# Score products of cached sample keys with both operands split into high and low parts, four tiles to a step, and four groups of instructions in other places

## The reference

```
h = rmsnorm(x, g_mix);  z = h @ w_in           # all heads and gates in one projection
mlstm: 4 heads;  dilated attention (dsa): 3 groups of 2 heads;  moba: 6 heads of 64
sample sequence:  s = q @ concat(cached k, new k).T / 8 + bias;  o = softmax(s) @ concat(cached v, new v)
x = x + merge(branches) @ w_out;  x = x + SwiGLU(rmsnorm(x)) @ w_down;  y = rmsnorm(x)
```

## Time and profile before

| | |
|---|---|
| median of 3 runs | 998.3 us (997.5 to 999.62) |
| profiled execution | 997.17 us, of which span 995.4 us |
| TensorE busy, products / weight loads | 98% / 95% of the span |
| VectorE, ScalarE, GpSimd busy | 49%, 34%, 8% |
| HBM read and written | 98.00 MB and 15.45 MB, 114 GB/s over the span |
| mean granted TensorE clock | 0.998 |

### The profile page before, as it was taken

The page is one execution under the profiler, slowest core; times in us unless marked ns, Lnnn a source line. Parts: engine busy times, 40 slices in busy tenths (PEclk is TensorE's granted clock), DMA queues, the critical chain, the costliest instruction groups (busy, mean ns, idle before and its releaser), DMA issues.

```text
span 995.4 us, 18277 instructions
## 1 busy us (share of the span) xinstructions
PE 972.5 (98%) x7624; PEld 947.2 (95%) x7624; DVE 487.0 (49%) x886; ACT 337.5 (34%) x577; POOL 75.6 (8%) x106
## 2 busy tenths in 40 slices
PE   6999999999999999999999999999999999999998
PEld 5899989999889899999999999999999999999997
DVE  5735566444886122645355565555445555323232
ACT  7443233444553441322222342222222222222122
POOL 0100022011301100111113000000000000000000
PEclk9999999999999999999999999999999999999999
DMA  7586437322321764222222222222223222222302
GB/s 251 149 251 235 76 90 152 114 81 78 103 60 35 224 196 114 84 86 86 85 86 85 86 85 86 85 86 88 94 96 98 94 85 75 86 74 76 116 2 90
DMA packets 104909, 105.03 MB, mean 106 GB/s; under 512 B 11130, under 2 KB 101752, under 8 KB 104492
## 3 DMA queue, kind: packets, MB, share of 16 engines
q1 hardware_dynamic: 101224, 92.78, 30.3%
q0 software_dynamic: 3552, 11.08, 3.6%
...
HBM read 98.00 MB, written 15.45 MB: 114 GB/s over the span
## 4 chain that ended last, share of the span: by engine, by line
PE 89%; DVE 5%; issue 1%; ACT 1%; POOL 1%; SPq 1%; DMA 1%; ACTq 0%; DVEq 0%; POOLq 0%
PE acc L451 75%; PE acc L1108 2%; PE acc L1057 1%; PE acc L1033 1%; PE acc L1144 1%; POOL mt L830 1%; DVE w_lo L435 1%; PE acc L1091 1%; PE acc L911 1%; PE acc L900 1%; SPq L681 1%; PE acc L871 1%; PE acc L1017 1%; DVE h_lo L2069 1%; PE acc L1232 1%
## 5 line engine op out<-in xcount | busy, mean ns | idle before, releaser
L451 PE MATMUL acc<-h_hi,w_hi 128*128 128x256 f32 (+1 forms) x1520 | 465.1, 306 | 2.1 <-DVE w_lo L435 1.6
L451 PE MATMUL acc<-h_lo,w_hi 128*128 128x256 f32 (+1 forms) x1520 | 437.7, 288 | 0.0
L451 PE MATMUL acc<-h_hi,w_lo 128*128 128x256 f32 (+1 forms) x1520 | 435.8, 287 | 0.0
L451 PEld LDWEIGHTS acc<-h_hi,w_hi 128*128 128x128 f32 x1520 | 285.8, 188 | 10.3 <-issue 4.2
L430 ACT ACTIVATE w_hi<-raw 128x1024 fp32r<-128x1024 f32 x135 | 141.4, 1047 | 441.7 <-PE acc L451 441.6
L451 PEld LDWEIGHTS acc<-h_lo,w_hi 128*128 128x128 f32 x1520 | 286.1, 188 | 4.8 <-issue 2.4
L451 PEld LDWEIGHTS acc<-h_hi,w_lo 128*128 128x128 f32 x1520 | 286.1, 188 | 0.0
L435 DVE TENSOR_TENSOR w_lo<-raw,w_hi 128x1024 fp32r<-128x1024 f32 x135 | 165.3, 1225 | 112.5 <-ACT w_hi L430 107.8
L451 PE MATMUL acc<-s_hi,w_hi 128*128 128x256 f32 (+1 forms) x352 | 101.6, 288 | 0.0
L451 PE MATMUL acc<-s_lo,w_hi 128*128 128x256 f32 (+1 forms) x352 | 101.3, 288 | 0.0
L451 PE MATMUL acc<-s_hi,w_lo 128*128 128x256 f32 (+1 forms) x352 | 100.7, 286 | 0.0
...
## 6 DMA issues: line engine op xcount, KB each, us to landing
raw<-in_w_in SPq DMA_DIRECT2D x25, 1024.0 KB, 5.1
raw<-in_w_gate_up SPq DMA_DIRECT2D x22, 1024.0 KB, 4.9
raw<-in_w_down SPq DMA_DIRECT2D x8, 1024.0 KB, 4.8
...
ring<-in_cache_dsa_kv SPq DMA_DIRECT2D x4, 1024.0 KB, 6.7
raw<-in_w_out SPq DMA_DIRECT2D x4, 1024.0 KB, 4.7
...
ring<-in_cache_moba_k SPq DMA_DIRECT2D x48, 64.0 KB, 2.1
```

Of the source, the lines that this page charges most:

```text
L451: ins = nc.tensor.matmul(acc[:, bank, 0:HALF[half]], a[:, k, :], two(b[:, kx + k, :], half), start=first and k == k0 and c == 0, stop=last ...
```

## The change

Sample keys. `Qpad` becomes fp32r and holds the high part of the queries in columns 0 to 63 and the low part in 64 to 127. ScalarE copies the transposed keys, now 512 columns (four tiles) at a time, into fp32r (`kt_hi`), and VectorE subtracts for the low part (`kt_ev`), in one of two buffers `KTs`. Each sequence takes two fp32r products, one with the high and one with the low keys. 22 steps stand in place of 48, transposes two steps ahead, over three banks. The low half of the scores is copied by ScalarE (`sample_low`) and added by VectorE (`sums`). The probabilities get a buffer `Ppad` of their own, which GpSimd clears once the keys phase is over. The products with `vn` go behind those with the cached values, and the result is copied in two pieces and turned by six transposes of 64 columns.

Gates. Block 0 takes two passes: its low weights stand in columns 64 to 127 of the high block; VectorE copies the rows from 64 on and adds them. Its load is narrower.

Places. `split_hi(0)` and `split_lo(0)` go ahead of the first activations; ScalarE's exp and ln for the gates go from 1.4 to 2.1; `T_F` goes from 29.1 to 29.35, and with it the mLSTM factors on VectorE; the copies of the shifted caches (`moved_up`) go from blocks 6, 7, 8 to 66, 70, 74. In the tail the products with the squares are taken apart, with four transposes between them, ahead of some waits.

```diff
-        Qpad = m("Qpad", [P, 2, NB, P])
+        Qpad = m("Qpad", [P, 2, NB, P], F32R)
...
-        KTs = Map(a_s + 8192, 2048)("KTs", [P, 2, 256])
+        Ppad = Map(a_b)("Ppad", [P, 2, NB, P])
+        KTs = [Map(a_a + 9216, 4096)("KTs0", [P, 2, 512], F32R), Map(sq_at, 4096)("KTs1", [P, 2, 512], F32R)]
...
-        loads.append(([(0, 0, rows(w_in, 0, KD, 1024, 32)), (0, 32, rows(w_in, 0, KD, 1028, 96))], P))
+        loads.append(([(0, 0, rows(w_in, 0, KD, 1024, 32)), (0, 32, rows(w_in, 0, KD, 1028, 32))], P))
...
+            c = HD if w == 0 else P
...
+            if w == 0:
+                both = split_block(w_hi, w)
+                nc.vector.tensor_tensor(both[:, :, HD:P], raw_block(w)[:, :, 0:HD], both[:, :, 0:HD].bitcast(F32),
+                                        ALU.subtract).then_inc(w_lo_done, 1)
+                return
...
+                passes = ((hi, x_hi), (hi, x_lo)) if w == 0 else ((hi, x_hi), (hi, x_lo), (lo, x_hi))
...
-        T_SA, T_F = 33, 29.1
-        T_QK, D_QK = 1.3, 0.042
+        T_SA, T_F = 33, 29.35
+        T_QK, D_QK = 1.3, 0.09
...
+        k_steps = [(m, range(b, b + 4 // NC4[q])) for m, q in enumerate(Q_ORDER) for b in range(0, NB, 4 // NC4[q])]
+        k_ends = [max(n for n, step in enumerate(k_steps) if step[0] == m) + 1 for m in range(6)]
+        K_BANK = (2, 6, 7)
+
+        def scores4(q):
+            return acc[:, 3 + q % 3, 2 * P * (q // 3):2 * P * (q // 3 + 1)]
...
-                    for g in range(3):
-                        yield 6 + g
...
-                                sp.wait_ge(sem("kt_tr"), NB * (n - 3))
+                                sp.wait_ge(sem("kt_tr"), k_ends[n - 4])
...
+                    for g in range(3):
+                        yield 66 + 4 * g
...
+                pool.wait_ge(sem("qk4"), len(k_steps))
+                set_to(Ppad[:, :, :, :], 0.0, "ppad")
...
-                        m, b = divmod(n, NB)
+                        m, batches = k_steps[n]
...
-                        if n >= 2:
-                            pe.wait_ge(sem("kt_ev"), n - 1)
+                        if n >= 3:
+                            pe.wait_ge(sem("kt_ev"), n - 2)
                         tiles, done, count = ring_tiles("k", q)
                         pe.wait_ge(done, count)
-                        for c in range(NC4[q]):
-                            ins = nc.tensor.transpose(acc[:, 6 + n % 2, P * c:P * (c + 1)], tiles[:, NC4[q] * b + c, :], ident)
+                        for c in range(4):
+                            ins = nc.tensor.transpose(acc[:, K_BANK[n % 3], P * c:P * (c + 1)], tiles[:, NC4[q] * batches[0] + c, :], ident)
                         ins.then_inc(sem("kt_tr"), 1)
...
-                    yield T_SA + T_QK
+                    yield T_SA + T_QK - 0.05
...
+                    pe.wait_ge(sem("new_ev"), 1)
                     turn_k(0)
-                    for n in range(6 * NB):
-                        m, b = divmod(n, NB)
+                    turn_k(1)
+                    for n, (m, batches) in enumerate(k_steps):
                         q = Q_ORDER[m]
                         yield T_SA + T_QK + n * D_QK
-                        if n + 1 < 6 * NB:
-                            turn_k(n + 1)
+                        if n + 2 < len(k_steps):
+                            turn_k(n + 2)
                         pe.wait_ge(sem("kt_ev"), n + 1)
-                        if b == 0:
+                        if batches[0] == 0:
                             pe.wait_ge(sem("qpad_done"), m + 1)
                         w = P * NC4[q]
-                        nc.tensor.matmul(acc[:, 3 + q % 3, 2 * P - w:2 * P], Qpad[:, q // 3, b, :], KTs[:, n % 2, 0:w],
-                                         start=b == 0 and q % 3 not in [o % 3 for o in Q_ORDER[:m]],
-                                         stop=b == NB - 1 and q % 3 not in [o % 3 for o in Q_ORDER[m + 1:]]).then_inc(sem("qk4"), 1)
+                        for i, b in enumerate(batches):
+                            for c in range(2):
+                                ins = nc.tensor.matmul(scores4(q)[:, 2 * P - w:2 * P], Qpad[:, m % 2, b, :], KTs[n % 2][:, c, w * i:w * (i + 1)],
+                                                       start=b == 0 and c == 0, stop=b == NB - 1 and c == 1, skip_group_check=True)
+                        ins.then_inc(sem("qk4"), 1)
...
-                    for q in range(6):
...
+                            ins = nc.tensor.matmul(out4(q), Ppad[:, j % 2, b, :], tiles[:, NC4[q] * b + c, :],
+                                                   start=b == 0 and j in (0, 4), stop=False, skip_group_check=True)
                         ins.then_inc(sem("pv_mm"), 1)
+                    pe.wait_ge(sem("ptn_ev"), 1)
+                    for q in range(6):
+                        half, g = divmod(q, 3)
+                        ins = nc.tensor.matmul(out4(q)[0:HD], PTn[:, g, HD * half:HD * (half + 1)], vn[:, P * q:P * (q + 1)],
+                                               start=False, stop=q in (3, 5), skip_group_check=True)
+                    ins.then_inc(sem("pv_mm"), 1)
...
+                    pe.wait_ge(sem("ob_ev"), 2)
+                    for q in range(6):
+                        ins = nc.tensor.transpose(acc[:, 3, HD * q:HD * (q + 1)], o_smp[:, q, :], ident[0:HD, 0:HD])
...
                 pe.wait_ge(sem("ssq3_done"), KD - 1)
+                for i in range(NT + 1):
+                    n = out_rows(i)
...
+                pe.wait_ge(acc_ev, n_sum - 2)
+                pe.wait_ge(sem("xg_done"), KD - 1)
+                y_turned(0, range(4))
+                pe.wait_ge(sem("sq3_done"), KD)
+                for i in range(NT + 1):
+                    n = out_rows(i)
+                    ins = nc.tensor.matmul(acc[0:n, 7, i:i + 1], sq[:, (KD - 1) % 2, P * i:P * i + n], ones[:, 0:1],
...
+                ins.then_inc(sem("rt_mm"), 1)
+                y_turned(0, range(4, KD - 1))
+                pe.wait_ge(sem("xg_done"), KD)
+                y_turned(0, range(KD - 1, KD)).then_inc(sem("y_tr"), 1)
                 pe.wait_ge(acc_ev, n_sum)
...
-                    yield 1.4
+                    yield 2.1
...
+                    yield T_SA + 0.75
+                    act.wait_ge(sem("new_mm"), 1)
+                    nc.scalar.copy(new_s[:, :, :], acc[:, 2, 0:3 * TS].rearrange("p (g n) -> p g n", n=TS)).then_inc(sem("new_ev"), 1)
+                    for n in range(len(k_steps)):
+                        yield T_SA + T_QK + (n - 1.8) * D_QK
                         act.wait_ge(sem("kt_tr"), n + 1)
                         if n >= 2:
                             act.wait_ge(sem("qk4"), n - 1)
-                        w = P * NC4[Q_ORDER[n // NB]]
-                        nc.scalar.copy(KTs[:, n % 2, 0:w], acc[:, 6 + n % 2, 0:w]).then_inc(sem("kt_ev"), 1)
+                        nc.scalar.copy(KTs[n % 2][:, 0, :], acc[:, K_BANK[n % 3], :]).then_inc(sem("kt_hi"), 1)
...
+                def sample_low():
...
+                        nc.scalar.copy(low_s[0:HD, g, c:2 * P], scores4(g)[HD:P, c:2 * P]).then_inc(sem("low_ev"), 1)
+                        nc.scalar.copy(low_s[HD:P, g, :], scores4(3 + g)[0:HD]).then_inc(sem("low_ev"), 1)
...
-                    nc.scalar.copy(S4[:, :, 0:P], acc[:, 7, 0:3 * P].rearrange("p (g n) -> p g n", n=P)).then_inc(sem("ob_ev"), 1)
+                    act.wait_ge(sem("pv_mm"), len(pv) + 1)
+                    nc.scalar.copy(o_smp[:, 0:4, :], acc[0:HD, 7, :].rearrange("p (q n) -> p q n", n=P)).then_inc(sem("ob_ev"), 1)
+                    nc.scalar.copy(o_smp[:, 4:6, :], acc[0:HD, 6, 0:2 * P].rearrange("p (q n) -> p q n", n=P)).then_inc(sem("ob_ev"), 1)
...
                 act.wait_ge(sem("vecs_done"), 1)
+                split_hi(act, 0)
                 x_hi(0)
...
-                split_hi(act, 0)
...
-                            v.do(nc.vector.tensor_tensor(two(i_row, half), src[0:HA], r[0:HA], ALU.mult))
-                            v.then(nc.vector.tensor_tensor(two(f_row, half), src[32:32 + HA], r[32:32 + HA], ALU.mult))
+                            both = two(v_st[:, 0, :], half)
+                            v.then(nc.vector.tensor_copy(both[0:36], src[HD:HD + 36]))
+                            v.then(nc.vector.tensor_tensor(both[0:36], src[0:36], both[0:36], ALU.add))
+                            v.do(nc.vector.tensor_tensor(two(i_row, half), both[0:HA], r[0:HA], ALU.mult))
+                            v.then(nc.vector.tensor_tensor(two(f_row, half), both[32:32 + HA], r[32:32 + HA], ALU.mult))
...
+                            p = HD * h
+                            q_new = qT[p:p + HD, 2 + q, TP:T].rearrange("p (b t) -> p b t", t=TB)
+                            v.do(nc.vector.tensor_tensor(parts[2 * h + 1], q_new, parts[2 * h].bitcast(F32), ALU.subtract))
...
+                def keys_low():
+                    for n in range(len(k_steps)):
+                        yield T_SA + T_QK + (n - 1.2) * D_QK
```

(14 more changed lines are left out.)

127 lines of the change are left out of this document (69 added, 58 removed).

## The result

993.6 us, the median of 7 runs, against 998.15 of before (7 runs): ratio 0.9946, 95% interval 0.9925 to 0.9967 (the ratios in this text are those on record, worked out from the single runs; the two medians alone give 0.9955). The single runs lie from 989.4 to 996.8 us, wider than those of before (997.0 to 999.6), and the profiled one is the slowest of them (996.81, span 995.0). So its trace shows the changed kernel at its worst, and it takes the experiments to tell the steady part of the change from the scattered one.

A forecast was written before the change was run, and what follows sets the result against it. TensorE, busy for 98% of the span, was taken as the bound. Terms of -0.5, -0.7, -5.7, +0.7, 0 and -1.1 sum to -7.3 us: 989.9 profiled, 991.0 as median; range 986.3 to 995.0.

The forecast's parts named there:

- its own case: Keys phase: loads pace it, as the terms were summed; 991.0 us, chance 0.58.
- (c): Keys phase: TensorE's clock falls behind new waits of 1 to 3 us; 993 to 994.6 us, chance 0.15.
- (d): Keys phase: the chain copy, subtraction, product binds over two buffers, 1.9 us a step; 994 us, chance 0.07.
- Start: First blocks: earlier low parts and fewer TensorE waits outweigh four more VectorE operations; -0.5 us, bounds -1.1 and +1.0.
- Attention: Attention: moved factors free VectorE where TensorE waits 1.9 us for PTs; about a third gained, -0.7 us.
- Keys phase: Sample keys' scores: cheaper fp32r products, partly lost to waits for loads; ends at 363.9 instead of 369.6, -5.7 us.
- After the keys: Behind the keys: extra copies of the result, a second VectorE copy and more small transposes cost +0.7 us.
- Cache copies: SyncE's queue, from blocks 6 to 8 to 66 to 74: no TensorE wait for weights at either place, 0.
- Tail: Behind the last block: half of the sums and four transposes ahead of or between waits; -1.1 us, clock gain uncounted.
- Rival (b): Keys phase: loads keep up; 987 us, or 985.5 with the tail's clock kept up as well; chance 0.13.

The follow-up runs named there:

- whole_again: The changed kernel run once more with no edit, for its spread and a second profile: 993.99 us, ratio 0.9954.
- gates_three: The changed kernel with block 0's gates in three passes as before, its splits still early: 990.72 us, ratio 0.9921.
- lo2_first: The changed kernel with block 2's w_lo on VectorE moved ahead of the gate rows' four new operations: 990.05 us, ratio 0.9917.
- keys_one_dma: lo2_first with each moba pair's keys loaded by one DMA instead of 16 by the page table: 988.63 us, ratio 0.9901.

## Why the prediction was right or wrong

The forecast was 991.0 with 989 to 993 for its own case and 986.3 to 995.0 over the rivals; 993.6 is inside the outer range and beyond the inner one. It is inside because the range had been stretched for rivals (c) and (d), and (c) came in at a place that the forecast hadn't thought of: that part is luck. By its steps:

- **Start, -0.5: failed.** The waits were sized well: w_lo of block 2 at 28.79 (forecast 29.2), block 2 on TensorE at 30.07 (30.4), the 2.85 us of VectorE's idle time gone. What I left out is that the clock can fall behind the 1.5 us wait. I had put such a fall (rival c) into the keys phase, at 1.9 us each; it cost some 3.5 at block 2, and in the keys phase the clock stayed at 1.00 behind waits of up to 1.66 us (1.73 in whole_again). The median, 993.6, is where rival c ends, by another place, and not every execution has the fall. Without the wait and the fall, the start gives -1.5 (gates_three) to -2.4 us (lo2_first) at block 5; with both, +2.2 and +2.7 in the two profiles.
- **Attention, -0.7: not there.** Block 28 to 34 moved by -0.61, +0.34, +0.42 and -0.48 us in the four profiles of the table with the factors moved, and by -0.68 to +0.81 in the six others. The lead is given back one block later, in a wait for PTs near 280 us that the kernel before doesn't have there; what sets its length stays open.
- **Keys phase, -5.7: right.** The end came 6.1 us sooner, 5.7 of them by the phase itself. The loads cost 4.4 us where 5.5 were forecast, and keys_one_dma shows that SyncE's issues are behind 3.6 of them. The sum came out better than its parts: pairs 3, 2 and 5 cost 3.0 us together instead of 5.5, and 1.26 us for pair 1 made up for part of it, which is luck. (In the other four profiles of the table that have the change in the keys, the sum is 4.3 to 4.7 us, with other shares.) Products are spaced as the block's own. The 128-column form, for which only bounds stood, takes 0.115 us, so pair 0 gained nothing. The estimate of 0.107 us as a floor, worked out from the load time in the Trainium skill ("TensorE: Matmul & The Clock Gate", LDWEIGHTS (loading the stationary operand)), agrees with this trace, where no distance of that form lies below it.
- **After the keys, +0.7: mis-sized.** From the 6.1 us at the phase's end 4.2 are left at block 40, +1.9, or +1.5 without the three block products that changed sides. The waits there:

```profile
PE acc L1168 <- DMA ring<-in_cache_moba_v: 1.5, 1, 1.5
PE acc L466 <- DVE gs L1656: 1.5, 1, 1.5
PE acc L1168 <- DVE Ppad L2143: 0.5, 1, 0.5
PE acc L1180 <- ACT o_smp L1498: 0.4, 1, 0.4
```

  against 1.1 and 1.6 in the earlier trace rows and 0.2 each for PTn and the result's copy: 0.7 us more in all. The wait for values is 0.4 us longer. SyncE's queue did move with TensorE, 3.3 us sooner at this load as TensorE at its wait, but from its first issue to the landing it takes 11.5 us instead of 11.1. The first copy into Ppad, priced at 0.2 with a bound of 0.4, shows 0.5. What I had left out is TensorE's own work: the twelve products with vn take 1.45 us in their new place instead of 1.07, the value products 0.1 more (the small transposes take 0.2 more, as priced).
- **Cache copies, 0:** not shown to be wrong; 0.9 us lies inside the intervals.
- **Tail, -1.1: right in TensorE's time** (1.15 us against the last block, at either clock), about 2 us by medians, and in single executions lost in the stores. I had counted none of the clock's part, and rightly: the fall comes in either order, and it costs 1.7 us, not the 1.9 that rival (c) took from it. (Rival (b)'s lower end should read 984.9 by the forecast's own terms, 986.8 less 1.9; nothing hangs on it.)

The sum then reads: keys and after -4.2 to -4.6, tail -1.15 by TensorE's time and about -2 by the medians, start -1.5 to -2.4 or, with the wait and the fall, +2.2 and more. Without the fall these make about 990 to 991, which lo2_first and gates_three have; the changed kernel lies between 989.4 and 998.3, in part by the falls it catches. Not all of its spread is the clock: 989.37 us was run at a mean clock of 0.998 and 992.56 at 0.999.

The version that beats both kernels is the change with one instruction moved, lo2_first: 990.05 and 989.54 us in two sets, ratio 0.9917 and 0.9915.
